# Moving the second memory's key and value projection from the first mixer to the second

## The reference

```
# first block, once
mem_kv = rmsnorm(mem, mem_norm) @ w_mem_kv          # 256 x 1024 @ 1024 x 512
# second block, in its mixer
mkv = rms_norm(mem_2, g_mem_2) @ w_mem_kv_2         # 256 x 1024 @ 1024 x 512
mk, mv = split(mkv); mk = rms_norm(mk per head)
y_mem = softmax(mq @ mk^T) @ mv                     # needed in the third mixer only
```

## Time and profile before

| | us |
|---|---|
| median of three runs (2084.0 to 2084.86) | 2084.2 |
| the profiled execution | 2083.41 |
| its span, first to last instruction | 2081.6 |
| PE busy | 2055.7 (99%) |
| DVE busy | 1280.0 (61%) |
| ACT busy | 962.2 (46%) |
| POOL busy | 50.5 (2%) |

### The profile page before, as it was taken

One profiled execution on the slowest core, in us unless ns is written; L12 is line 12 of the kernel. 1 busy time (PEld: TensorE's weight loads), 2 busy tenths in 40 slices (PEclk: granted clock), 3 DMA queues, 4 the chain that ended last, 5 costly groups with the idle time before them and its releaser, 6 DMA issues.

```text
span 2081.6 us, 29983 instructions
## 1 busy us (share of the span) xinstructions
PE 2055.7 (99%) x11114; PEld 1730.2 (83%) x11114; DVE 1280.0 (61%) x2086; ACT 962.2 (46%) x1880; POOL 50.5 (2%) x95
## 2 busy tenths in 40 slices
PE   7999999999999899999999999999999999999999
PEld 7999888888889788888888888888889778888887
DVE  7655677637754787875577544344548985544442
ACT  7755554424445875543344433223344664322331
POOL 0000001000000110000000000000001100000000
PEclk9999999999999999999999999999999999999999
DMA  6222233333332011333333333333332123333332
GB/s 206 80 63 61 62 93 100 97 96 97 97 94 87 19 46 55 98 97 96 97 98 100 97 95 98 97 96 97 96 96 72 37 77 96 96 97 96 97 97 90
DMA packets 101666, 185.53 MB, mean 89 GB/s; under 512 B 11408, under 2 KB 14864, under 8 KB 101264
## 3 DMA queue, kind: packets, MB, share of 16 engines
q1 hardware_dynamic: 101520, 183.61, 30.2%
HBM read 181.47 MB, written 2.10 MB: 88 GB/s over the span
## 4 chain that ended last, share of the span: by engine, by line
PE 92%; DVE 4%; ACT 2%; issue 1%; SPq 0%; DMA 0%; DVEq 0%; ACTq 0%
PE PSA L1905 25%; PE PSA L1907 25%; PE PSA L1906 25%; PE PSA L1923 3%; PE PSA L1925 3%; PE PSA L1924 3%; PE PSA L2037 2%; PE PSA L2023 2%; PE PSA L2011 1%; DVE PSTAT L2176 1%; ACT PP L2422 1%; PE PSA L1965 1%; DVE RS L2068 1%; DVE WL L2080 0%; PE PSA L2004 0%
## 5 line engine op out<-in xcount | busy, mean ns | idle before, releaser
L2352 ACT ACTIVATE WH<-RAW 128x512 fp32r<-128x512 f32 (+3 forms) x681 | 426.7, 627 | 811.0 <-PE PSA L1907 693.5
L2080 DVE TENSOR_TENSOR WL<-RAW,WH 128x512 fp32r<-128x512 f32 (+3 forms) x681 | 469.4, 690 | 398.4 <-ACT WH L2352 376.6
L1905 PE MATMUL PSA<-HNh,WH 128*128 128x512 f32 x1440 | 562.4, 391 | 0.0
L1907 PE MATMUL PSA<-HNh,WL 128*128 128x512 f32 x1440 | 560.3, 389 | 0.0
L1906 PE MATMUL PSA<-HNl,WH 128*128 128x512 f32 x1440 | 560.2, 389 | 0.0
L1906 PEld LDWEIGHTS PSA<-HNl,WH 128*128 128x128 f32 x1440 | 270.3, 188 | 57.2 <-issue 1.2
L1905 PEld LDWEIGHTS PSA<-HNh,WH 128*128 128x128 f32 x1440 | 270.3, 188 | 56.9 <-issue 1.2
L1907 PEld LDWEIGHTS PSA<-HNh,WL 128*128 128x128 f32 x1440 | 270.3, 188 | 56.3
L1905 PE MATMUL PSA<-Gh,WH 128*128 128x512 f32 x704 | 273.9, 389 | 0.0
L1906 PE MATMUL PSA<-Gl,WH 128*128 128x512 f32 x704 | 273.9, 389 | 0.0
L1907 PE MATMUL PSA<-Gh,WL 128*128 128x512 f32 x704 | 273.9, 389 | 0.0
(11 more groups left out here) (252 smaller groups left out, 2244.9 us busy)
## 6 DMA issues: line engine op xcount, KB each, us to landing
RAW<-in_w SPq DMA_DIRECT2D x659, 256.0 KB, 2.6
XT<-in_x SPq DMA_DIRECT2D x8, 256.0 KB, 5.0
MT<-in_mem SPq DMA_DIRECT2D x2, 1024.0 KB, 6.1
out_x<-XT SPq DMA_DIRECT2D x8, 256.0 KB, 2.1
RAW<-in_w SPq DMA_DIRECT2D x8, 208.0 KB, 2.4
RAW<-in_w SPq DMA_DIRECT2D x6, 192.0 KB, 2.3
RAW<-in_w SPq DMA_DIRECT2D x8, 134.0 KB, 5.2
PAR<-in_par SPq DMA_DIRECT2D x1, 207.0 KB, 6.0
```

Of the source, the lines that this page charges most:

```text
L1905: pe.matmul(out, wh, xh, start=(a["start"] and c == 0), stop=False)
L1907: p = pe.matmul(out, wl, xh, start=False, stop=ends)
L2080: dve.tensor_tensor(l, r, h, ALU.subtract).then_inc(done.sem("split.dve"), 1)
L2352: act.activation(h, r, ACT.Copy).then_inc(done.sem("split.act"), 1)
```

## The change

The group ("mem", 1) is taken out of `FOX_GROUPS` and of the weight order, and `mem_kv(1, ...)` runs in the second mixer, after the wide group of the memory queries and before the side job is added. The order of the other groups stays. Its norm moves to the start of the first FFN, at the third pair of columns; the angle steps, which were there, come 34 beats later. The normed memory stands in UQ. Three waits follow from that: `rtab` waits for the last norm step that reads MT, the norm waits for the first mixer's last pair, and pair 1's turns wait for the group of the values in place of `g_mq`. The keys use the buffer YK before round 0 does, and the two groups use the banks 6 and 7.

```diff
-FOX_GROUPS = (("v", 0), ("qk", 0), ("mem", 1), ("qk", 1), ("v", 1), ...
+FOX_GROUPS = (("v", 0), ("qk", 0), ("qk", 1), ("v", 1), ...
     wide("mla", 0, (0, 128))
+    mem("w_mem_kv_2")
     for g in range(3):
...
+        def mem_parts_late(c):
+            s = slice(MEM * (c % 2), MEM * (c % 2) + MEM)
+            return tuple(x[:, c // 2, s] for x in UQ)
...
-            return [atts[0].last(1, "pscore.pe")] if c < 2 else [("dense", g_mem[1])] if c < 6 else []
+            return [atts[0].last(1, "pscore.pe")] if c < 2 else [("dense", g_mem[0])] if c < 6 else []
...
-            after(5, lambda: mem.columns(1 + m))
+            if not m:
+                after(5, lambda: mem.columns(1 + m))
...
-        mems[1].free = [("dense", g_mem[0])]
-        for c in range(KC):
-            after(8 + 2 * c, lambda c=c: mems[1].feed(c, ("mem", 1)))
...
+        def memory():
+            mems[1].free = [atts[0].last(7, x) for x in ("pscore.pe", "pvals.pe")]
+            for c in range(KC):
+                after(3 * c, lambda c=c: mems[1].feed(c, ("mem", 1)))
+            after(30, lambda: mems[1].columns(2))
+            after(34, angles)
...
-            after(48, lambda: step("rtab", 0, A=TMP[i]))
+            after(48, lambda: step("rtab", 0, A=TMP[i], before=[
+                (x, ("mem1", KC - 1)) for x in ("part.act", "part.dve", "square.act")]))
...
-        ffn(0, "ffn_w_up", "ffn_w_up", "ffn_w_down", 0, FF, last, True, 1.0, norm, angles)
+        ffn(0, "ffn_w_up", "ffn_w_up", "ffn_w_down", 0, FF, last, True, 1.0, norm, memory)
...
+        aux_ring[:] = [0, 1, 2, 3]
+        mem_kv(1, mems[1], (6, 7), take_memory)
         pair_got = [[] for _ in range(6)]
...
-            w, free = places[p % 2], [("dense", g_mq)] if p < 2 else [att.last(2 + p - 2, "pscore.pe")]
+            w, free = places[p % 2], [("dense", (g_mq, g_mem[1])[p])] if p < 2 else [att.last(2 + p - 2, "pscore.pe")]
```

More of the change, by code:

```diff
@@ L39 @@
 LAT_COLS = (384, 512, 640, 256)
-FOX_GROUPS = (("v", 0), ("qk", 0), ("mem", 1), ("qk", 1), ("v", 1), ("qk", 2), ("qk", 3), ("v", 2), ("qk", 4),
+FOX_GROUPS = (("v", 0), ("qk", 0), ("qk", 1), ("v", 1), ("qk", 2), ("qk", 3), ("v", 2), ("qk", 4),
               ("qk", 5))
@@ L107, in weight_plan @@
     for what, p in FOX_GROUPS:
[L108 to L111, removed]
+        wide("fox", 0, fox_cols(what, p))
     opened("w_out", 0, OUT_ORDER, rows(0, 4) + out_parts(4, 7))
@@ L1497, in program @@
         mems = [Norm("mem0", MT, "memn", MEM, ACCM[0], [], mem_parts),
-                Norm("mem1", MT, "memn2", MEM, ACCM[1], None, mem_parts)]
+                Norm("mem1", MT, "memn2", MEM, ACCM[1], None, mem_parts_late)]
         for c in range(KC):
@@ L1542, in program @@
             banks, two = halved([0, 1])
-            if what == "mem":
-                mem_kv(1, mems[1], (0, 1), take_y(YB, 1))
-            elif what == "v":
+            if what == "v":
                 for x in range(2):
@@ L1617, in program, with take_memory @@
                           for y in YQ], 1), halves=2, lag=1)
+        yk = Slots(1, need)
+        def take_memory(g):
+            yk.take(g, [("qturn.pe", (g, 1))])
+            return YK[:, :, :].rearrange("p a b -> p (a b)")[:, 0:1024].rearrange("p (t c) -> p t c", t=4), yk.before[g]
+        aux_ring[:] = [0, 1, 2, 3]
+        mem_kv(1, mems[1], (6, 7), take_memory)
         pair_got = [[] for _ in range(6)]
@@ L1631, in program @@
         M = [RS[x][:, :].rearrange("p (a b) -> p a b", b=32) for x in range(2)]
-        yk = Slots(1, need)
         def turn_pair(gq, gk, yq, yk_, p, ends):
-            w, free = places[p % 2], [("dense", g_mq)] if p < 2 else [att.last(2 + p - 2, "pscore.pe")]
+            w, free = places[p % 2], [("dense", (g_mq, g_mem[1])[p])] if p < 2 else [att.last(2 + p - 2, "pscore.pe")]
             def go(x):
@@ L2549, in gpsimd @@
                     w.wait_ge(s_par, 16)
+                    for t in a["before"]:
+                        w.wait_ge(*done(*t))
                     pool.tensor_scalar(NS, CS[:, 1, :, :], -1.0, None, ALU.mult).then_inc(g_in.sem, g_in.up())
```

## The result

Measured side by side, five rounds: before 2083.8 us (2082.9 to 2086.2, 11 runs), after 2089.4 us (2089.1 to 2091.1, 11 runs). The ratio after to before is 1.0027, 95% interval 1.0018 to 1.0035, so the change costs 5.6 us. The forecast was 2082.2 us with a range up to 2088: wrong side, and outside the range. In the profiled executions the spans are 2081.6 and 2087.7 us.

What follows compares the result with a forecast made beforehand. PE, busy for 99% of the span, was taken as the bound, with ACT's load holding it back before pair 0. -12.3 + 12.3 - 2.0 = -2.0 us gave a median of 2082.2 us, range 2076 to 2088.

Steps and rivals of the forecast that it cites:

- PE work removed: First mixer: the group's 96 matmuls, norm totals and turns come off a PE without gaps, -12.3 us.
- PE work added: Second mixer: same instructions and shapes, +12.3 us; weights keep up, with 1.6 us as the bound if they don't.
- The norm, moved into the first FFN: First FFN: the norm's added DVE and ACT work costs 0 us, bounds 0 and 4 us.
- DVE's backlog: First FFN: a few us are worked off; in rival D (4%) 7 us reach the weight splits, +4 us.
- The fill: Second mixer, up-projection to pair 0: 28.3 us instead of 30.3, gain 2.0 us, ends 0 and 8.3.
- Rival C: Second mixer: memory attention beside the up-projection uses cover too early, chain stands bare; +4.7 us, median 2088.9; chance 16%.
- rival A: Second mixer: side job beside the up-projection covers softmax latency; -4.2 to -8.3 us, at -6.3 median 2077.9; chance 31%.
- The ceiling of 8.3 us: All the second mixer can give back: 6.0 us gaps, 0.8 later, 1.5 for the low clock.
- B: Second mixer: PE's busy rows hide short waits, so more than visible gaps returns; -10 us, 2074.2; chance 5%.
- The estimate worked out from the latter: Second mixer: 8.3 and 9.5 us slack by weight-load share against the first mixer's 90%; sum up to -17.8 us.

Runs made afterwards that it cites:

- the held kernel: Changed kernel with the second mixer's side job (memory attention) added only behind all of round 0's up-projection; 2083.2 us, ratio to before 0.9995.
- with the bank set too: Changed kernel with the memory attention held behind round 0's up-projection and the first FFN's last down-projection tile put into PSUM bank 4; 2082.1 us, ratio 0.9991.
- the best version: Changed kernel with the last down tile in bank 4, the group behind round 0's up-projection and the memory attention added between the two; 2081.9 us, ratio 0.9990.
- the kernel with the group ahead of pair 1's turns: Changed kernel with the last down tile in bank 4 and the group moved behind round 0's up-projection, attention added as in the changed kernel; 2082.5 us, ratio 0.9991.
- the version with the attention behind the group: Changed kernel with the last down tile in bank 4, the group directly behind round 0's up-projection and the attention added behind the group; 2082.3 us, ratio 0.9992.

## Why the prediction was wrong

**PE work removed: right.** 12.3 forecast, 12.6 by the first FFN's start (11.8 to 12.8 over the ten kernels with that first mixer), with PE at 209.00 of 209.00 us in 50 to 259 of the changed kernel. By medians the second memory's removal is worth 11.8. Nothing shows that the group was cover in the first mixer.

**PE work added: right.** From the latents' group to the up-projection's start it takes 44.25 us against 31.61, so 12.6, with PE and clock full; 0.25 of it goes with the bank, which leaves 12.4. The weights keep up.

**The norm, moved into the first FFN: the size was off, by a term not in the list.** Forecast 0 with bounds 0 and 4; the FFN took 361.44 us against 359.94, so +1.5. DVE's backlog, which I weighed, never reached PE. The norm's column totals, which PE now does inside the FFN, are 0.5 us of it; the forecast had them in the second mixer's +12.3, so they were put in the wrong stage but not left out of the sum. What it left out is the rotation of PSUM banks: 1.0 us here and 0.25 behind it.

**The fill: the step that failed.** This term was put at -2.0 us and measured +4.6 (2.7 to pair 0, 1.9 behind it), most of what separates forecast and result. The forecast put up-projection to pair 0 at 28.3 us, "since ACT's row is the nearest thing to a measurement of the limit". It came out at 33.0, with 4.8 us free on ACT behind the up-projection. I had worked out ACT's load for the stretch (27.1 us; it is 27.02 in the changed kernel) and taken the load for the duration. The load was right to 0.1 us and the duration off by 4.7, because the order had changed: the memory attention was spent beside the up-projection, the keys' chain began 8.7 us later, and PE and ACT then had too little beside it. Holding the attention back gave 26.85 us, but with only 25.31 us of ACT's work in the stretch, since some of the attention now ran behind pair 0's first scores. Counted to the second FFN, where all of that is done, the held kernel takes 159.1 us, the kernel before 160.8 and the changed one 165.4. So the forecast gain of 2.0 us was there to have, 1.7 by this count, in the order that the forecast had silently assumed; with the bank set too, that kernel came out at 2082.1 us, beside a forecast of 2082.2.

**Rival C is what happened,** at 16% too cheap. Its price was +4.7 us; it measured +2.7 to pair 0 and +1.9 after it, where PE has 3.6 us of gaps against 2.3 before and the clock is low for the first 0.7 us. Its mechanism holds: the up-projection's end slipped from 7.9 to 16.5 us, and the chain stood behind it with too little cover. Its sizes were not all right: it put pair 0 20 us plus 15 behind the up-projection's start, and that came out as 16.3 plus 16.7, because part of the attention was left for later after all. That pair 0's +2.7 and the +1.9 behind it add up to the +4.7 of its price is in part luck. Of the two arguments against it, the first (ACT free for the chain) fell since the last copies queue behind exponentials, and the second (the pace leaves some) held only in part: all the memory's scores were out by 685.7, and the turns and value products that were left kept PE busy for 6.05 of 12.25 us. The rival's condition, that the memory queries are ready when the up-projection starts, is one that the change makes true: 12 us of other matmuls now stand between their projection and that start. I had used that condition for rival A and not asked in the forecast what it does to the order. In the two kernels where the attention is added ahead but the queries' projection stands right before the up-projection, the first memory score still came only behind it (664.97 and 665.72, last up-projection matmuls at 664.65 and 665.40).

**The ceiling of 8.3 us** counted 1.5 us for the low clock. No run shows that this can be had: the stretch to pair 0 takes 30.32 us with the clock low for 3.4 us of it and 30.32 us with the clock at 1.00 throughout.

**Rivals A and B** supposed that cover placed before the gaps would fill them. Held back, the attention leaves 26.85 us to pair 0, close to A's "under 26", but 1.8 of the 3.5 us gained there were only work put off: from pair 0 to the second FFN it takes 132.25 us against 130.45, and PE's gaps are no larger (2.1 us against 2.3), its work is (130.18 us against 128.17).

The Trainium skill (Perfetto Trace Analysis, Identifying the Most-Contended Engine) judges PE's headroom by the share of peak arithmetic reached and by the busy share of the weight loads. The estimate worked out from the latter in the prediction, with the first mixer's share as the goal, was up to 17.8 us to win; the best version won 3.0 us in that mixer, so the little weight given to it fits, though no run shows that more was not to be had.

## What to carry to other kernels

When work is moved in front of a dependent chain, ask not only what load each engine has, but which filler work becomes ready earlier, and whether it is spent before the chain begins: one line that holds the filler back was worth 6.2 us here, and 12 us of additional filler on top of it nothing that could be measured (2081.9 to 2082.5 us against 2082.1). An engine's load over a stretch is a lower bound for it, not its duration. A step moved across a stage also shifts rotating buffers and banks behind it, so list which bank the next stage finds busy. And compare orders at a point where the same work is done in both: a step that comes earlier may only have jumped the queue.

## What was not expected of the hardware

In the changed kernel the granted clock fell to 0.50 within the 3.14 us gap and stayed there for 6.8 us; in the kernel with the group ahead of pair 1's turns it was 0.50 for 5 us and more behind gaps of 2.17 and 1.69 us (PE busy for 1.92 of 5.00). In the version with the attention behind the group, whose single gaps are at most 1.00 us, it stayed at 1.00.

The same kernel doesn't always get the same clock. The kernel before was timed 75 times beside the experiments: with a mean clock of 1.000 (16 runs) the median is 2083.4 us, with 0.999 (19 runs) 2083.1, with 0.998 (35 runs) 2084.4, with 0.997 (4 runs) 2085.8 and with 0.996 (one run) 2087.3. All 11 runs of the changed kernel have 0.998. So the same fall of the clock cost nothing in the stretch of 30.32 us, where PE had gaps that the slower matmuls could fill, and some 2 us in the 3.95 us behind the long gap, where PE was busy throughout.
